# Causal mask of the second attention on VectorE, in one pass with the row's extreme, instead of on TensorE

## What is computed

```python
log_f = jax.nn.log_sigmoid(f_logit + b_forget[l])
cum = jnp.cumsum(log_f, axis=1).transpose(0, 2, 1)
o_b = block_attention(qf, kf, vf, fox_scale, frame_mask, cum)

def block_attention(q, k, v, scale, diag_mask, cum=None):
    for q0 in range(0, S, Q_BLOCK):                       # 4 blocks of 128 queries
        s = einsum('bhqd,bhkd->bhqk', q[q0:q1], k[:q1]) * scale
        if cum is not None:
            s = s + cum[q0:q1, None] - cum[None, :q1]
        s = where(mask, s, -inf)                          # only the last 128 keys are masked
        p = softmax(s, axis=-1)
        outs.append(p @ v[:q1])
```

## Time and profile before

| | |
|---|---|
| time, median of 3 runs | 1800.88 us (1800.87 to 1801.72) |
| span of the profiled execution, first to last instruction | 1799.4 us |
| profiled execution's own time | only its span is shown; the median of the runs is 1.5 us above it |
| busy: PE, DVE, ACT, POOL | 1744.6, 1086.1, 672.7, 166.0 us |
| steps 32 to 63 of the attention stage | about 225 to 332 us (first layer), 1103 to 1210 us (second layer) |
| mean granted clock of TensorE | 0.995 |

### The profile page before, as it was taken

The page is one execution under the profiler, slowest core; times in us unless marked ns, Lnnn a source line. Parts: engine busy times, 40 slices in busy tenths (PEclk is TensorE's granted clock), DMA queues, the critical chain, the costliest instruction groups (busy, mean ns, idle before and its releaser), DMA issues.

```text
span 1799.4 us, 22083 instructions
## 1 busy us (share of the span) xinstructions
PE 1744.6 (97%) x7877; PEld 1376.7 (77%) x7877; DVE 1086.1 (60%) x1647; ACT 672.7 (37%) x1125; POOL 166.0 (9%) x125
## 2 busy tenths in 40 slices
PE   5999999999999999999999999999999999999998
PEld 4777666777888888888878766668778888888886
DVE  7688778767555555543348878768665555555322
ACT  4454444434333332222235444444343432322222
POOL 3220000010020000001121200000100200000010
PEclk8999999999999999999999999999999999999999
DMA  4432111233333333333333311113334333333331
GB/s 123 103 85 63 47 48 48 65 88 94 94 106 95 102 93 93 101 88 97 94 89 70 100 47 48 48 36 95 88 89 115 94 95 103 95 93 95 92 97 68
DMA packets 308469, 152.21 MB, mean 85 GB/s; under 512 B 30436, under 2 KB 307166, under 8 KB 308396
## 3 DMA queue, kind: packets, MB, share of 16 engines
q1 hardware_dynamic: 308096, 151.05, 30.3%
q10 hardware_dynamic: 300, 0.19, 0.0%
HBM read 149.09 MB, written 2.10 MB: 84 GB/s over the span
## 4 chain that ended last, share of the span: by engine, by line
PE 84%; DVE 11%; ACT 3%; issue 2%; DMA 0%; SPq 0%; ACTq 0%; DVEq 0%
PE bank L1271 64%; PE bank L1346 11%; PE bank L1328 3%; PE bank L1379 2%; PE bank L1358 2%; DVE w_lo L891 2%; DVE c_acc L951 1%; ACT w_hi L602 1%; DVE q_t L978 1%; DVE h_lo L920 1%; DVE k_t L981 0%; DMA x_rows<-in_x 0%; DVE tmp L912 0%; PE bank L1296 0%; DVE c_raw L1100 0%
## 5 line engine op out<-in xcount | busy, mean ns | idle before, releaser
L602 ACT CAST w_hi<-raw 128x1024 fp32r<-128x1024 f32 (+4 forms) x330 | 301.5, 917 | 733.3 <-PE bank L1271 732.9
L891 DVE TENSOR_TENSOR w_lo<-raw,w_hi 128x1024 fp32r<-128x1024 f32 (+4 forms) x330 | 355.4, 1080 | 250.2 <-ACT w_hi L602 248.3
L1271 PE MATMUL bank<-h_hi,w_hi 128*128 128x512 f32 (+1 forms) x1200 | 474.3, 395 | 8.8 <-DVE w_lo L891 3.8
L1271 PE MATMUL bank<-h_lo,w_hi 128*128 128x512 f32 (+1 forms) x1200 | 468.0, 390 | 0.0
L1271 PE MATMUL bank<-h_hi,w_lo 128*128 128x512 f32 (+1 forms) x1200 | 467.8, 390 | 0.0
L1271 PEld LDWEIGHTS bank<-h_hi,w_hi 128*128 128x128 f32 (+1 forms) x1200 | 224.9, 187 | 67.4 <-issue 11.6
L1271 PEld LDWEIGHTS bank<-h_lo,w_hi 128*128 128x128 f32 (+1 forms) x1200 | 225.0, 188 | 48.9 <-issue 2.5
L1271 PEld LDWEIGHTS bank<-h_hi,w_lo 128*128 128x128 f32 (+1 forms) x1200 | 224.9, 187 | 48.4
L912 DVE TENSOR_TENSOR tmp<-bank,rstd_x 128x512 f32<-128x512 f32 x140 | 96.7, 690 | 264.2 <-PE bank L1271 259.3
L951 DVE SCALAR_TENSOR_TENSOR c_acc<-u_pad,dwk_l,c_acc 128x512 f32<-128x512 f32 x240 | 173.9, 746 | 1.1
L502 POOL TENSOR_TENSOR x_acc<-x_acc,x_sq 128x512 f32<-128x512 f32 x39 | 66.8, 1712 | 881.8 <-ACT x_sq L612 549.1
(11 more groups left out here) (203 smaller groups left out, 2133.6 us busy)
## 6 DMA issues: line engine op xcount, KB each, us to landing
raw<-in_w_in SPq DMA_DIRECT2D x96, 512.0 KB, 3.8
raw<-in_w_ffn_gate SPq DMA_DIRECT2D x44, 512.0 KB, 3.8
raw<-in_w_ffn_up SPq DMA_DIRECT2D x44, 512.0 KB, 3.8
raw<-in_w_ffn_down SPq DMA_DIRECT2D x32, 512.0 KB, 3.8
raw<-in_w_out SPq DMA_DIRECT2D x16, 512.0 KB, 3.8
raw<-in_w_ffn_down SPq DMA_DIRECT2D x16, 384.0 KB, 3.3
raw<-in_w_bo_a SPq DMA_DIRECT2D x16, 256.0 KB, 2.8
raw<-in_w_bo_b SPq DMA_DIRECT2D x16, 256.0 KB, 2.8
```

What stands on the lines that cost most here:

```text
L602: last = nc.scalar.copy(to, of)
L891: last = nc.vector.tensor_tensor(to, of, part.bitcast(F32), ALU.subtract)
L1271: ins = nc.tensor.matmul(bank_t[0:rows, :], wt[slot][:, w], x, start=first and k == 0 and p == 0, stop=last and k == k_tiles - 1 and p == 2)
```

## The change

The queries of the second attention are scaled by a negative number, and the constant row that carries the cumulated forget sums is -1 instead of 1, so the scores come out negated. The mask product is left out for these 64 steps (32 in each layer). DVE takes the minimum over the columns before the last block (`low_part`, only where q > 0), waits for it, and adds a mask of 0 and +1e30 to the last 128 columns in PSUM in one instruction that also takes the minimum, beginning from `low_part`. ACT's exponential takes the scores with scale -1. The first attention is as before. The mask's second half is written by an instruction of its own at the start.

```diff
-OWN = 1 + 1 + 4 + 2 + STEPS + DT + 1 + FT
+OWN = 1 + 1 + 4 + 2 + STEPS + STEPS // 2 // TT * (TT - 1) + DT + 1 + FT
+    low_part = sb("low_part", [P, 4])
-                        nc.gpsimd.memset(q_t[NOPE:NOPE + 1, 2 * pair:2 * pair + 2, :], 1.0).then_inc(ones_put, 1)
+                        nc.gpsimd.memset(q_t[NOPE:NOPE + 1, 2 * pair:2 * pair + 2, :], -1.0).then_inc(ones_put, 1)
                     nc.scalar.activation(p_b[:, P_AT[s % 4]:P_AT[s % 4] + w], s_bank[s % 4][:, 0:w], ACT.Exp,
-                                         bias=neg_max[:, s % 4:s % 4 + 1],
+                                         bias=neg_max[:, s % 4:s % 4 + 1], scale=(1.0, -1.0)[pair // PAIRS],
                                          accum_out=row_sum[:, s % 4:s % 4 + 1]).then_inc(exp_done, 1)
-    ins = nc.vector.scalar_tensor_tensor(q_t[0:NOPE, 2 * pair + e, :], stat_bank[rows, :], FOX_SCALE,
+    ins = nc.vector.scalar_tensor_tensor(q_t[0:NOPE, 2 * pair + e, :], stat_bank[rows, :], -FOX_SCALE,
                                          rstd_x[rows, :], ALU.mult, ALU.mult)
                     q = g % 4
-                    nc.vector.tensor_reduce(neg_max[:, q:q + 1], s_bank[q][:, 0:(q + 1) * P], AX_X, ALU.max,
-                                            negate=True).then_inc(max_ready, 1)
+                    row, diag = s_bank[q], s_bank[q][:, q * P:(q + 1) * P]
+                    if g < STEPS // 2:
+                        nc.vector.tensor_reduce(neg_max[:, q:q + 1], row[:, 0:(q + 1) * P], AX_X, ALU.max,
+                                                negate=True).then_inc(max_ready, 1)
+                    else:
+                        if q:
+                            mine(nc.vector.tensor_reduce(low_part[:, q:q + 1], row[:, 0:q * P], AX_X, ALU.min))
+                        nc.vector.tensor_tensor_reduce(diag, diag, mask_b[:, 1, :], 1.0, low_part[:, q:q + 1] if q else -MASKED, ALU.add, ALU.min,
+                                                       neg_max[:, q:q + 1]).then_inc(max_ready, 1)
-            nc.vector.tensor_copy(mask_b[:], const_sb[:, P:3 * P].rearrange("p (m k) -> p m k", m=2)).then_inc(const_ok, 1)
+            nc.vector.tensor_copy(mask_b[:, 0, :], const_sb[:, P:2 * P]).then_inc(const_ok, 1)
+            nc.vector.tensor_scalar(mask_b[:, 1, :], const_sb[:, 2 * P:3 * P], -1.0, None, ALU.mult).then_inc(const_ok, 1)
-                    nc.tensor.matmul(s_bank[q][:, 0:w], q_t[0:rows, head, q * P:w], k_t[0:rows, head, 0:w], start=True, stop=True)
-                    nc.tensor.matmul(s_bank[q][:, q * P:w], ident_b[:], mask_b[:, kind, :], start=False, stop=True,
-                                     skip_group_check=True).then_inc(score_done, 1)
+                    ins = nc.tensor.matmul(s_bank[q][:, 0:w], q_t[0:rows, head, q * P:w], k_t[0:rows, head, 0:w], start=True, stop=True)
+                    if kind == 0:
+                        ins = nc.tensor.matmul(s_bank[q][:, q * P:w], ident_b[:], mask_b[:, 0, :], start=False, stop=True, skip_group_check=True)
+                    ins.then_inc(score_done, 1)
-            pe.wait_ge(const_ok, 3)
+            pe.wait_ge(const_ok, 4)
```

## The result

| | before | after |
|---|---|---|
| time, median | 1801.07 us (4 runs, 1800.87 to 1801.72) | 1812.15 us (4 runs, 1811.68 to 1813.17) |
| ratio after / before | | 1.0061, 95% interval 1.0049 to 1.0072 |
| span of the profiled execution | 1799.4 us | 1810.3 us |

What follows compares the result with a forecast made beforehand. PE was taken to bound the kernel (busy 97% of the span), with DVE able to spoil it. PE's 3.62 us a layer less 2.35 us of waits gave 1.27, 2.5 in both: 1798.4 us, range 1795.3 to 1808.0.

Steps and rivals of the forecast that it cites:

- Nothing moves on ACT, POOL or SP, no DMA is added: Second attention: beyond PE and DVE no engine gets other work; nothing counted for ACT's exponential behind DVE's new wait.
- the rivals: Whole kernel: slower, 1807.1 us (chance 0.23); faster, read hidden, 1796.6 us (0.16); PE's gain whole, 1793.7 us (0.01).
- The slower one: DVE, attention steps: accumulator read dear or masking instruction at half rate, 0.52 and 0.33 us a step, 1807.1 us; chance 0.23.
- The mask product, 0.113 us: PE, second attention: each mask product left out saves 0.113 us, 3.6 us in a layer if nothing else waits.
- PE's gain if DVE lost nothing, 2.9 us a layer: PE, second attention: with DVE losing nothing at all, 2.9 us gained in a layer, so 1795.1 us.
- DVE, 0.26 us a step with q > 0: DVE's reduction, masking and read in each step: 0.86 us against 0.60; with q = 0, 0.07 us more.
- The upper bound's 2.08 ns per column: DVE's masking instruction at the scan's rate: 0.42 us for 128 columns, 0.33 us to the next start.
- What DVE's delay costs: Second attention: DVE's 6.8 us a layer mostly swallowed by waits before `put`s; the rest delays PE at transposes.
- The places: PE's waits at transposes: 0.69 us in step 49, 0.64 in 54, 0.47 over steps 31, 38, 41, 43.
- Together: PE and DVE terms carried through a layer's steps: 1.27 us gained in a layer, 2.5 us in both.
- The profile it asked for: Signs expected in the profile after, all in the second attention stage, such as each stretch 1.3 us shorter.
- The rule on DVE: DVE: counting each instruction in full makes a step 0.35 or 0.16 us dearer; 0.2 us gained a layer, 1800.6 us.

Runs made afterwards that it cites:

- b3: The change with its new buffer allocated behind the region, no address moved, but PE's mask product kept for all steps, against the kernel before: 1803.50 us, ratio 1.0013.
- b4: Kernel before, changed to mask on DVE in one instruction over the whole row with a wide mask, no `low_part`, no address moved: 1797.24 us, ratio 0.9975.
- d1: Kernel before with every SBUF buffer 32 bytes further on, all distances between buffers kept: 1801.20 us, ratio 1.0001.
- d2: Kernel before with 32 unused bytes ahead of the weights' buffers, so weights and everything behind them move and `h` doesn't: 1821.93 us, ratio 1.0115.

## Why the prediction was wrong

**The step that failed** is "Nothing moves on ACT, POOL or SP, no DMA is added", read as if it were the whole list of side effects. The forecast costed instructions and left the diff's new buffer out altogether. The trace of before gave no hint: its products on f and on `h` stand at the same distance (487 in 110 us, 443 in 100 us, both 226 ns). What the runs show in its place: 32 bytes ahead of the region cost 11.0 us (2.18 + 2.13 + 3.50 + 3.20), shown by a2, which has those bytes and nothing else (1812.77 us), and by b1, which has the change without them (1799.56 us). How the place of the buffer acts on PE stays open. None of the rivals had this mechanism. The slower one was about DVE, and its 1807.1 us would have been near the result for a wrong reason; the masking instruction didn't run at half rate.

**The change that was costed** came out at 1799.56 us (b1) where the forecast had 1798.4, that is 1.6 us gained against 2.5. Term by term:
- *The mask product, 0.113 us:* measured 0.110 in 25 steps. Right.
- *PE's gain if DVE lost nothing, 2.9 us a layer:* measured 2.36 in the layer without a fall of the clock. Of the 0.5 us, 0.3 are the three places above (at two of them a wait was covered by a record and had no idle time to be read, at the third transposes follow), 0.1 the 3 ns a step, and 0.1 the mask product of step 63, which the forecast counts and which lies behind the end of the measured stretch.
- *DVE, 0.26 us a step with q > 0:* measured 0.26, though from other terms. The masking instruction is recorded with 0.359 us instead of 0.286 and the read costs 0 instead of 0.07; the two errors are equal and opposite, so that the sum is right is luck. With q = 0, 0.02 us instead of 0.07. (The upper bound's 2.08 ns per column is the scan's 1217 ns less the 153 ns that a reduction has beyond its columns, over 512 columns; the forecast doesn't say so.)
- *What DVE's delay costs:* forecast 2.9 - 1.27 = 1.6 us a layer beside PE's gain, measured 2.36 - 0.95 = 1.4. Alone it costs 1.0 (b3, where 0.9 was expected). The places were right: step 41 (idle time from 0.14 to 0.41 us, 0.26 forecast), step 49 (0.57 us, 0.69 forecast) and step 54 (0.30 us, 0.64 forecast).
- *Together:* 0.95 us a layer instead of 1.27.

**The profile it asked for.** Of its signs most came, some smaller than forecast: no bf16 product, each stretch shorter by 0.95 us (1.3 forecast), DVE busier by 5.1 to 6.1 us (6 to 9 forecast), the masking instruction at 0.293 us with q = 0 and 0.359 us else (near 0.29 forecast), the read below 0.16 us, DVE's wait before the gate tiles at 6.5 us in b1 (about 6 forecast; the 8.1 us of the kernel after are of the layer in which the clock fell, in its second layer it is 6.5 as well). The line of b1:

```profile
L970 DVE TENSOR_TENSOR q_t<-bank,rstd_x 128x512 f32<-128x512 f32 x6 | 4.1, 690 | 6.5 <-PE bank L1356 6.5
```

PE's wait before transposes went to 3.5 us, less than the 4 forecast. All these signs are about one stage, and all would have been there with any cost elsewhere: a list of what to look for should have had one line for the stages that the change leaves alone.

**The rule on DVE** that was weighed was that the next operation starts only when the pipe is empty. Here the masking instruction's record ends at 236.17 us and the next two start at 236.08, so the overlap of the earlier trace rows holds for this operation as well. The forecast took half of what the Trainium skill says (VectorE: DVE Perf Modes, The DRAIN you can't avoid): the same section adds "A next op that is not held starts earlier" (held: made to start only when every earlier one has finished). With that the trace agrees. The half rate of an instruction with two sources isn't seen either: with one source in PSUM and the other bf16, b4's rows stand within 10 ns of the plain reduction's. The Trainium skill (Vector Engine (DVE) Microarchitecture Reference, Points that are easy to get wrong) states it for one instruction layout with two non-bf16 sources in SBUF, and the masking instructions here have at most one such source.

## What to carry to other kernels

List a diff's allocations beside its instructions: a buffer of 32 bytes moved 91 KB behind it and cost 11.0 us where the change itself won 1.6, and an unused buffer of the same size in the old kernel is the run that shows it. Where products in a row set the time, keep the place of the streamed operand against the weights (here 256 bytes more did no harm), and look at the distance of starts or the count in a window in stages that the change doesn't touch. An added operand in a reduction over a whole row cost at most 10 ns on DVE, and cutting the row in two to save columns cost 0.26 us.

## What the runs showed of the hardware

- Products of 512 columns start 227 ns apart (mean over the first layer's down projection) where the streamed operand stands at its old place against the weights or 256 bytes further, and 233, 229, 233 and 233 ns apart at 32, 64, 96 and 128 bytes. That it is the weights, and not another buffer that moves with them, is inferred from d1 and d2. A shift of all buffers together changes nothing (1801.20 against 1801.15 us).
- Reading DVE's accumulator has a record of 143 ns, and the instruction behind it starts at the same moment as it does.
- A masking reduction that takes its start value from SBUF is recorded with 359 ns, one that takes it as a constant with 293 ns. The first kind also stands right behind a wait for the minimum; no run separates the two.
- Between 100 and 1780 us the granted clock fell to 0.50 for 3.4 us in 7 of the 17 profiled executions, always after the wait ahead of step 43's transposes, and cost 1.2 to 1.6 us; waits of 1.5 to 1.8 us stood there with and without a fall.
